# Two unused gaps in SBUF that move where a kernel's split activations begin

## The chip, the cores and the metric

The kernel runs on one core of one Trainium2 chip. The metric is the time of one execution on the device in microseconds (us), the median of several runs. Durations of single instructions are in nanoseconds (ns).

## What is computed

Two small transformer-like models in a row, two layers each, in float32, batch 1. The first has 256 tokens and 16 learned tokens ahead of them (272 in all), the second the 256 alone; the width is 1024. A layer is a mixer (gated linear attention, a sparse attention, a gated recurrence, a banded attention) and a feed-forward block. The change touches the operands of three products:

```python
def swiglu(h, w_in, w_out):                  # both layers of the first model, D_FF = 2816
    gate, up = jnp.split(h @ w_in, 2, axis=-1)
    return (jax.nn.silu(gate) * up) @ w_out

# the end of gla_mixer, layer 0 of the first model
    o = rmsnorm(o, g_out.reshape(GLA_HEADS, GLA_DV)).astype(h.dtype).reshape(B, T, D_MODEL)
    return (o * jax.nn.silu(r)) @ w_out
```

## The kernel before

Activations lie transposed in SBUF: the 128 partitions hold features, the free dimension holds tokens, and a tensor of 1024 features is eight rows one behind the other in each partition. Weights come as a stream of units of 128x1024 numbers (512 KB) through a ring of four slots, in the order in which they are used (`PHASES`).

**Split products.** To keep float32 accuracy, each operand of a large product is split into a high part of type float32r and a low part, the rest. ScalarE makes `w_hi` from `w_raw` (L511), VectorE makes `w_lo` (L1679), and the activations are split likewise. Each 128x128 tile of a unit then takes three matmuls with the weights as the stationary and the activations as the moving operand:

```python
wh = w_hi[:, slot, n * P:(n + 1) * P]
wl = w_lo[:, slot, n * P:(n + 1) * P]
nc.tensor.matmul(out, wh, xh[:, k, tok], start=first and n == 0, stop=False)   # L1004
nc.tensor.matmul(out, wh, xl[:, k, tok], start=False, stop=False)              # L1005
ins = nc.tensor.matmul(out, wl, xh[:, k, tok], start=False, ...)               # L1006
```

One unit is 24 such matmuls. `xh` and `xl` are `x_hi` and `x_lo` for most products, and tensors of their own for others:

- `ga_hi`, `ga_lo`: the gated output of the linear attention, 8 rows (k) of 272 tokens, made at L617 and L1860, read by the product `gla_out`: 8 rows x 3 matmuls x 8 output tiles = 192 matmuls of 272 columns.
- `mid_hi`, `mid_lo`: the middle of the gated feed-forward block, 22 rows, made tile by tile at L653 and L1905 while the first product of the block still runs, read by `ffn0_out` (272 columns) and `ffn1_out` (256 columns): 22 x 3 x 8 = 528 matmuls in each of the two layers.
- `m_hi`, `m_lo` (the second model's feed-forward blocks), `at_*`, `xq_*`, `c_*`, `lr_*` alike.

**Where things lie.** SBUF tensors are laid out one behind the other in each partition, each size rounded up to 32 bytes. What is used in one stage only lies in a region that every stage reuses from the same address (`region()`): one for the linear attention, one for the gated feed-forward block, one for the sparse attention, and so on. So a tensor's place follows from the sizes ahead of it in its own region. Tensors named `..._pad` are never read or written. The rows of `x`, `ga` and `mid` are 320 numbers (1280 bytes, five times 256) apart, of which 272 or 256 are used, so that every row starts at the same place past a multiple of 256 bytes; those of `m`, `at`, `xq` and `lr` are 1024 bytes apart. Two exceptions: row 7, the last of `x_hi` and `x_lo`, lies 64 bytes further, and the rows of `c_hi` and `c_lo` are 1088 bytes apart. `xs_hi` is the same tile as `x_hi` with the 256 tokens' first at the row's start; where `x_hi` itself is read for the 256 tokens alone, reading begins 64 bytes further, past the 16 learned tokens. In the program as built this gives, for the moving operands, in bytes past a multiple of 256:

| operand | columns | start |
|---|---|---|
| `mid`, `ga` | 272 or 256, 272 | 64 |
| `m`, `at`, `xq` | 256 | 64 |
| `x` in the first model's full products (rows 0 to 6; row 7) | 272 | 64; 128 |
| `xs` (rows 0 to 6; row 7) | 256 | 64; 128 |
| `x` in `dsa_qidx` and `dsa_q` (rows 0 to 6; row 7) | 256 | 128; 192 |
| `c_hi`, rows 0 and 1 (L1274, L1276) | 272 | 64, 128 |
| `c_lo`, rows 0 and 1 (L1275) | 272 | 192, 0 |
| `k2rs_hi`, `k2rs_lo` (L1500, L1501) | 256 | 96 |

The stationary operands `w_hi` and `w_lo` start 128 bytes past a multiple of 256, tile by tile 512 bytes apart.

**Order.** Every engine's order is written out by hand, with semaphores between the engines. TensorE waits for `lo_ready` (weights split) and for the activations' split at a stage's start, ScalarE and VectorE wait for `units_used` and `acc_free`, by which TensorE gives back a ring slot and an output bank is handed on, and SP reloads a slot when VectorE has split it.

Of the kernel before, what the change touches and what calls it, by code (L numbers as in the profile page):

```python
# [21 lines left out]
P = 128  # L22
# [131 lines left out]
def build(nc, hT, weights, cols, w_a2, bias1_rows, bias2_rows, constants, outT):  # L154
    ctx = ExitStack()
    with ctx:
# [37 lines left out]
        def region():  # L194
            stack = ExitStack()

            def get(name, shape, dt=F32):
                return stack.enter_context(nc.sbuf_tensor(name, shape, dt))
            return stack, get


        stack, get = region()
        ga_hi = get("ga_hi", [P, KD, ROW], F32R)
        ga_lo = get("ga_lo", [P, KD, ROW], F32R)
        k_T = get("k_T", [P, 4, T])
# [21 lines left out]
        stack, get = region()  # L227
        gate_s = get("gate_s", [P, 2, T])
        up_s = get("up_s", [P, 2, T])
        silu_s = get("silu_s", [P, 2, T])  # L230
        mid_s = get("mid_s", [P, 2, T])
        mid_hi = get("mid_hi", [P, 24, ROW], F32R)
        mid_lo = get("mid_lo", [P, 24, ROW], F32R)
        sqg = get("sqg", [P, KD, T])
# [3 lines left out]
        stack, get = region()  # L238
# [30 lines left out]
        stack, get = region()  # L269
# [15 lines left out]
        stack, get = region()  # L285
# [7 lines left out]
        stack, get = region()  # L293
# [2244 lines left out]
def program(nc, arrays):  # L2538
    args = [nc.dram_tensor(n, a.shape, mybir.dt.from_np(a.dtype), kind="ExternalInput").ap()
            for n, a in arrays.items()]  # L2540
    out = nc.dram_tensor("outT", (P, KD, SEQ), F32, kind="ExternalOutput").ap()
    build(nc, *args, out)
# [12 lines left out]
```

## Time and profile before

| | before |
|---|---|
| median of 3 runs | 1182.88 us |
| runs | 1182.33 to 1183.76 us |
| span of the profiled execution | 1182.2 us |
| PE busy | 1169.6 us, 99% |
| DVE busy | 819.2 us, 69% |
| ACT busy | 691.5 us, 58% |
| DMA | 207.84 MB, mean 176 GB/s |

The profiled execution has no time of its own beside its span; the span lies 0.7 us under the median of the runs. PE is TensorE's matmuls, PEld its weight loads, DVE VectorE, ACT ScalarE, POOL GpSimd. Matmuls are pipelined, so the records of successive ones overlap: a matmul's record is about 163 ns longer than the distance from its start to the next one's start. The distance is what one matmul costs in a stream.

### The profile page before, as it was taken

What the parts mean: (1) busy time and instruction counts of PE and PEld (TensorE: products, weight loads), DVE (VectorE), ACT (ScalarE), POOL (GpSimd) and SP (SyncE); (2) the same over time, 40 slices, a digit from 0 to 9 for tenths busy, and PEclk for the clock granted to TensorE, in tenths of its full rate; (3) what the DMA queues carried; (4) which work ended last, traced back from release to release, by engine and by line L of the source; (5) the groups of instructions that cost most, each with busy time, mean ns of one, the idle gap of its engine ahead of it and who ended that gap; (6) DMA issues with size and microseconds to landing.
All of it is one profiled execution on the core that took longest, in us unless ns stands there. A gap on an engine that the chain in (4) does not pass through costs nothing. (4 is left out here: it accounts for less than half of the span.)

```text
span 1182.2 us, 25988 instructions
## 1 busy us (share of the span) xinstructions
PE 1169.6 (99%) x9738; PEld 1140.9 (97%) x9738; DVE 819.2 (69%) x1296; ACT 691.5 (58%) x1115; POOL 89.5 (8%) x97
## 2 busy tenths in 40 slices
PE   8999999999999999999999999999999999999998
PEld 8999999999998899999999989999999979999998
DVE  7767866665577877666668997675567677776543
ACT  6635765654455567666556976664447576666432
POOL 1000200000110020000120000000013223000000
PEclk9999999999999999999999999999999999999999
DMA  7532655555664336555664556666666424566663
GB/s 270 177 94 89 193 178 177 177 178 192 200 202 144 107 107 190 191 190 193 209 209 155 193 180 192 191 193 191 206 212 205 142 77 153 185 193 193 202 195 106
DMA packets 57577, 207.84 MB, mean 176 GB/s; under 512 B 6352, under 2 KB 7568, under 8 KB 57248
## 3 DMA queue, kind: packets, MB, share of 16 engines
q1 hardware_dynamic: 57136, 203.52, 54.6%
q0 software_dynamic: 288, 3.21, 0.7%
q8 instruction: 54, 0.88, 0.3%
q14 instruction: 19, 0.16, 0.0%
q10 hardware_dynamic: 80, 0.07, 0.0%
HBM read 205.66 MB, written 1.05 MB: 175 GB/s over the span
## 5 line engine op out<-in xcount | busy, mean ns | idle before, releaser
L1679 DVE TENSOR_TENSOR w_lo<-w_raw,w_hi 128x1024 fp32r<-128x1024 f32 x379 | 463.4, 1225 | 68.7 <-ACT w_hi L511 68.1
L511 ACT CAST w_hi<-w_raw 128x1024 fp32r<-128x1024 f32 x379 | 395.1, 1045 | 174.1 <-PE acc L1006 172.2
L1004 PE MATMUL acc<-x_hi,w_hi 128*128 128x256 f32 (+1 forms) x1688 | 479.0, 284 | 2.2 <-DVE w_lo L1679 1.5
L1005 PE MATMUL acc<-x_lo,w_hi 128*128 128x256 f32 (+1 forms) x1688 | 473.3, 280 | 0.0
L1006 PE MATMUL acc<-x_hi,w_lo 128*128 128x256 f32 (+1 forms) x1688 | 473.2, 280 | 0.0
L1004 PEld LDWEIGHTS acc<-x_hi,w_hi 128*128 128x128 f32 x1688 | 317.8, 188 | 6.0 <-DVE x_lo L1699 1.8
L1005 PEld LDWEIGHTS acc<-x_lo,w_hi 128*128 128x128 f32 x1688 | 317.7, 188 | 0.5
L1006 PEld LDWEIGHTS acc<-x_hi,w_lo 128*128 128x128 f32 x1688 | 317.6, 188 | 0.0
L1004 PE MATMUL acc<-m_hi,w_hi 128*128 128x256 f32 x512 | 141.3, 276 | 0.0
L1005 PE MATMUL acc<-m_lo,w_hi 128*128 128x256 f32 x512 | 141.3, 276 | 0.0
L1006 PE MATMUL acc<-m_hi,w_lo 128*128 128x256 f32 x512 | 141.3, 276 | 0.0
L1004 PE MATMUL acc<-mid_hi,w_hi 128*128 128x272 f32 (+1 forms) x352 | 99.0, 281 | 0.0
L1006 PE MATMUL acc<-mid_hi,w_lo 128*128 128x272 f32 (+1 forms) x352 | 99.0, 281 | 0.0
L1005 PE MATMUL acc<-mid_lo,w_hi 128*128 128x272 f32 (+1 forms) x352 | 99.0, 281 | 0.0
L1006 PEld LDWEIGHTS acc<-m_hi,w_lo 128*128 128x128 f32 x512 | 96.1, 188 | 0.0
L1004 PEld LDWEIGHTS acc<-m_hi,w_hi 128*128 128x128 f32 x512 | 96.1, 188 | 0.0
L1005 PEld LDWEIGHTS acc<-m_lo,w_hi 128*128 128x128 f32 x512 | 96.1, 188 | 0.0
L1006 PEld LDWEIGHTS acc<-mid_hi,w_lo 128*128 128x128 f32 x352 | 66.2, 188 | 0.0
L1004 PEld LDWEIGHTS acc<-mid_hi,w_hi 128*128 128x128 f32 x352 | 66.2, 188 | 0.0
L1005 PEld LDWEIGHTS acc<-mid_lo,w_hi 128*128 128x128 f32 x352 | 66.2, 188 | 0.0
L887 ACT ACTIVATE y_s<-y_s 128x256 f32<-128x256 f32 x64 | 26.8, 419 | 63.3 <-DVE y_s L2304 62.9
L526 ACT ACTIVATE sq<-h 128x256 f32<-128x256 f32 (+1 forms) x64 | 26.3, 420 | 57.9 <-DVE h L1714 47.8
(370 smaller groups left out, 1671.3 us busy)
## 6 DMA issues: line engine op xcount, KB each, us to landing
w_raw<-weights SPq DMA_DIRECT2D x381, 512.0 KB, 4.0
bias<-bias_rows POOLq DMA_DIRECT2D x1, 2048.0 KB, 8.7
h<-hT SPq DMA_DIRECT2D x4, 272.0 KB, 4.5
bias<-bias_rows POOLq DMA_DIRECT2D x1, 1088.0 KB, 8.9
outT<-h SPq DMA_DIRECT2D x4, 256.0 KB, 4.6
con<-constants SPq DMA_DIRECT2D x1, 913.0 KB, 9.3
w_raw<-weights SPq DMA_DIRECT2D x2, 256.0 KB, 3.1
par<-cols SPq DMA_DIRECT2D x1, 84.0 KB, 2.0
```

Of the source, the lines that this page charges most:

```text
L511: nc.scalar.copy(w_hi[:, slot, :], w_raw[:, slot, :]).then_inc(hi_ready, 1)
L526: nc.scalar.activation(sq[:, nn, tok], h[:, nn, tok], ACT.Square).then_inc(sq_ready, 1)
L887: nc.scalar.activation(y2_s[:, j % 2, :], y_s[:, j % 2, :], ACT.Square).then_inc(s_("y2_ready"), 1)
L1004: nc.tensor.matmul(out, wh, xh[:, k, tok], start=first and n == 0, stop=False)
L1005: nc.tensor.matmul(out, wh, xl[:, k, tok], start=False, stop=False)
L1006: ins = nc.tensor.matmul(out, wl, xh[:, k, tok], start=False, stop=last and n == ntiles - 1)
L1679: V.tensor_tensor(w_lo[:, slot, :], w_raw[:, slot, :], w_hi[:, slot, :].bitcast(F32), ALU.subtract)\
```

## The change

Two tensors that nothing uses are put into two of the regions. `ga_pad` takes 32 bytes in each partition at the start of the linear attention's region, `mid_pad` 128 bytes in the feed-forward region, between `mid_s` and `mid_hi`.

```diff
         stack, get = region()
+        ga_pad = get("ga_pad", [P, 8])
         ga_hi = get("ga_hi", [P, KD, ROW], F32R)
         ga_lo = get("ga_lo", [P, KD, ROW], F32R)
         k_T = get("k_T", [P, 4, T])
...
         mid_s = get("mid_s", [P, 2, T])
+        mid_pad = get("mid_pad", [P, 32])
         mid_hi = get("mid_hi", [P, 24, ROW], F32R)
         mid_lo = get("mid_lo", [P, 24, ROW], F32R)
         sqg = get("sqg", [P, KD, T])
```

No instruction is added, removed or moved on any engine; only addresses differ. In the built program `mid_hi` and `mid_lo` start at 192 past a multiple of 256 instead of 64, and `sqg` behind them moves by the same 128 bytes. `ga_hi` and `ga_lo` start at 96 instead of 64, and all that lies behind them in the linear attention's region (`k_T`, `v_T`, `q_T`, `r_T`, `a1_T`, `z` and its fellows, `k_tok`, `v_tok`, `S`, `o_T` and so on) moves by 32 bytes. The other regions, the weights' ring and `x` stay where they were.

## Rows read from the trace of the kernel before

**Rows 1.** The page's part 1: busy us, share of the span, instructions.
```profile
PE 1169.6 (99%) x9738; PEld 1140.9 (97%) x9738; DVE 819.2 (69%) x1296; ACT 691.5 (58%) x1115; POOL 89.5 (8%) x97
```

**Rows 2.** Windows, PE alone: stretch, length, busy (instructions in it), clock, DMA.
```profile
core 0: us, PE busy (x), PEclk, DMA share, GB/s
270.00:330.00 60.00, 60.00 (x488) 1.00 0.62 197
567.00:622.00 55.00, 55.00 (x488) 1.00 0.66 211
119.00:134.00 15.00, 15.00 (x124) 1.00 0.68 221
150.00:260.00 110.00, 110.00 (x890) 1.00 0.57 177
450.00:560.00 110.00, 110.00 (x966) 1.00 0.59 188
800.00:870.00 70.00, 70.00 (x620) 1.00 0.63 193
```

**Rows 3.** Groups of matmuls by line and shape: count | busy us, mean ns | idle before.
```profile
L1004 PE MATMUL acc<-mid_hi,w_hi 128*128 128x272 f32 x176 | 50.4, 287 | 0.0
...
L1004 PE MATMUL acc<-mid_hi,w_hi 128*128 128x256 f32 x176 | 48.6, 276 | 0.0
...
L1004 PE MATMUL acc<-ga_hi,w_hi 128*128 128x272 f32 x48 | 13.8, 286 | 0.0
```

**Rows 4.** Groups of all engines in the stretch of `ffn1_out`, 564.3 to 623.9.
```profile
L1679 DVE TENSOR_TENSOR w_lo<-w_raw,w_hi 128x1024 fp32r<-128x1024 f32 x24 | 30.2, 1281 | 2.5 <-ACT w_hi L511 2.5
L511 ACT CAST w_hi<-w_raw 128x1024 fp32r<-128x1024 f32 x24 | 25.0, 1047 | 14.0 <-PE acc L1006 14.0
...
L1714 DVE TENSOR_TENSOR h<-h,acc 128x256 f32<-128x256 f32 x7 | 3.0, 422 | 15.3 <-PE acc L1006 15.3
```

**Rows 5.** Timeline of PE in `dsa_qidx`: start us, length, engine, line, names.
```profile
343.63 0.28 PE L1004 MATMUL acc<-x_hi,w_hi 128*128 128x256 f32 x1
...
345.07 0.28 PE L1004 MATMUL acc<-x_hi,w_hi 128*128 128x256 f32 x1
...
345.43 0.29 PE L1004 MATMUL acc<-x_hi,w_hi 128*128 128x256 f32 x1
...
347.95 0.28 PE L1004 MATMUL acc<-x_hi,w_hi 128*128 128x256 f32 x1
```

**Rows 6.** Timeline of PE in `ffn0_in`, from row 7 of one unit on.
```profile
201.07 0.28 PE L1004 MATMUL acc<-x_hi,w_hi 128*128 128x272 f32 x1
...
201.45 0.29 PE L1004 MATMUL acc<-x_hi,w_hi 128*128 128x272 f32 x1
...
204.04 0.28 PE L1004 MATMUL acc<-x_hi,w_hi 128*128 128x272 f32 x1
```

**Rows 7.** Timeline of PE in the products of `c`; six matmuls from the first row to the last.
```profile
373.34 0.29 PE L1275 MATMUL acc<-c_lo,w_hi 128*128 128x272 f32 x1
...
374.08 0.29 PE L1275 MATMUL acc<-c_lo,w_hi 128*128 128x272 f32 x1
```

**Rows 8.** Timeline of PE where `k2rs` is spread; four matmuls to the last row.
```profile
920.19 0.29 PE L1500 MATMUL pa<-k2rs_hi,hbrd 128*128 128x256 f32 x1
...
920.67 0.28 PE L1004 MATMUL acc<-xq_hi,w_hi 128*128 128x256 f32 x1
```

**Rows 9.** Groups of matmuls in one unit of `q2`, 917.3 to 919.8.
```profile
L1004 PE MATMUL acc<-xq_hi,w_hi 128*128 128x256 f32 x8 | 2.2, 281 | 0.0
```

**Rows 10.** Groups of matmuls of the linear attention by line and shape, whole span.
```profile
L1135 PE MATMUL acc<-q_T,S 128*128 128x64 f32 x64 | 7.6, 271 | 0.0
...
L1122 PE MATMUL pa<-v_tok,k_tok 64*128 64x256 f32 x16 | 5.2, 477 | 0.2 <-DVE v_tok L1799 0.2
```

## The prediction

> **What bounds the kernel now.** The page's busy shares come first: TensorE is busy 99% of the span, VectorE 69%, ScalarE 58% [rows 1]. The kernel is a stream of matmuls, and its time is their number times the distance between two starts. The change adds no instruction, so I ask two things: is the distance set by TensorE itself in the three stages that read the moved operands, and does it depend on where the moving operand begins?
>
> For the first, windows over the two feed-forward output products and the linear attention's show PE busy for their whole length, at a granted clock of 1.00 (the level of 2.4 GHz) [rows 2]. The groups of `ffn1_out` show who waits: VectorE stood idle 15.3 us and ScalarE 14.0 us for TensorE's matmuls, and the matmuls have no idle time [rows 3, 4]. DMAs were busy 62 to 68% [rows 2]. So whatever a matmul gains or loses there goes into the span one to one, 528 times in each layer and up to 192 times in `gla_out`. Longer matmuls only make the two other engines wait longer; nothing behind them becomes late.
>
> The distances at the present start of 64 bytes follow from the windows, where about two of the counted instructions straddle an end: 60 us over 486 is 123.4 ns for `mid` with 272 columns, 55 over 486 is 113.2 ns for `mid` with 256, 15 over 122 is 123 ns for `ga`, and 70 over 618 is 113.3 ns for `m` [rows 2]. The bare columns at 2.4 GHz are 113.3 and 106.7 ns, so 10 and 6.6 ns come on top at this start.
>
> **The second question, from the rows that happen to start elsewhere.**
>
> 256 columns at 128 bytes: in `dsa_qidx` rows 0 to 6 of `x` start at 128. From 343.63 to 345.07 there are 12 matmuls: 120 ns each. Same line, same weights' place, same column count as the 113.2 ns at 64.
>
> 256 columns at 192 bytes, the new place of `mid`: row 7 of the same products. Its three matmuls take from 345.07 to 345.43, again 120 ns each, and the 24 of the next whole unit, from 345.07 to 347.95, are 2.88 us, 120 ns each with row 7 in them [rows 5]. If row 7 took 113 ns, 20 ns would be missing there. So 192 costs what 128 does: 6.7 ns more than 64.
>
> A second look at 128: the long stream of `xs` (450 to 560) has only row 7 at 128. 110 us over 964 is 114.1 ns on the mean, 0.9 more than 113.2; over 24 matmuls that is 21 ns, 7 for each of the three of row 7 [rows 2]. It agrees.
>
> 272 columns at 128 bytes: row 7 in `ffn0_in`. Its three matmuls take 0.38 us (127 ns each) [rows 6], and the window's mean of 110 over 888, 123.9 ns, against 123.4 gives 24 x 0.5 / 3 = 4 ns more for each [rows 2]. I take 127.
>
> 272 columns at 192: only `c_lo`'s first row. A run of six (two at 64, two at 128, one each at 192 and 0) takes 0.74 us [rows 7]. Less 2 x 123.4 and 2 x 127, there are 240 ns for the two at 192 and 0 together. If the one at 0 costs its bare columns, 113.3, the one at 192 costs 127; if both cost the same, 120. So the bounds are 120 and 127, or with the largest row for this shape, rounding in, 128. I take 126, near the upper end, because with 256 columns 192 costs as much as 128.
>
> 272 columns at 96: no row. It lies between 64 (123.4) and 128 (127). The nearest row is `k2rs` with 256 columns at 96: four matmuls in 0.48 us, 120 ns [rows 8], but in a stretch where operands at 64 run slow too (below). I take 2 ns more, bounds 0 and 4.
>
> **The sum.**
> - `ffn1_out`: 528 x 6.7 ns = 3.5 us. If the stream settles at the 118 ns of rows 9, 2.5.
> - `ffn0_out`: 528 x (126 - 123.4) = 1.4 us; bounds 528 x (-3.4) = -1.8 and 528 x 4.6 = 2.4.
> - `gla_out`: 192 x 2 ns = 0.4 us; bounds 0 and 0.8. Its first 48 matmuls wait for `ga_ready` anyway.
> - the linear attention's other operands, moved by 32 bytes: their main matmuls are 7.6 and 5.2 us [rows 10]; 6% of that, the largest effect of a start seen above, is 0.8 us either way. They lie among waits between engines. I take 0.
> - ScalarE's and VectorE's writes of `mid` and `ga` and GpSimd's reads of `sqg` start elsewhere too. I take 0: in the stages that use them TensorE is waited for, 14 to 15 us of it [rows 4], which is the cover; a tenth more on each would not use it up.
>
> Sum +5.3 us. The profiled span would go from 1182.2 to 1187.5, and since the runs' median stands 0.7 us above the span, the median from 1182.88 to 1188.2. The ends of the terms give 2.5 - 1.8 - 0.8 = -0.1 and 3.5 + 2.4 + 0.8 + 0.8 = 7.5: 1182.8 to 1190.4.
>
> **A rule that speaks against it.** The rows say that two streams of 256 columns in the same line differ by 6.7 ns with the start alone. The Trainium skill, page "TensorE: Matmul & The Clock Gate", section "Back-to-back issue gap", gives the distance as columns over 2.4 plus 2.5 ns, with no term for where the operand begins; by it nothing would change. Its page "SBUF — State Buffer", section "Door 1: The DMA port swizzle", has lines of 16 bytes, and 64, 96, 128 and 192 are all multiples of 16; by that too nothing would change. That is the second rival below, whose price is zero.
>
> **The rivals.**
> 1. *Another start is better for 272 columns (faster).* The run of `c` allows it: if a start at 0 costs 123.4 like one at 64, the one at 192 costs 117, and `ffn0_out` gains 528 x 6.4 = 3.4 us. Against the 3.5 us lost in `ffn1_out` that alone comes out even. It ends faster only if 192 with 256 columns costs less than 64 + 1.9 ns or so, that is, if row 7's 120 ns in rows 5 is only the neighbours' pace carried over, since three matmuls between two groups at 120 may not show their own cost. With 113.2 there the time is 1182.9 - 3.4 = 1179.5 us. For it: row 7 is never seen in a stream of its own. Against it: rows 5 has it to the nanosecond at 120, and in the stream of `xs` three odd matmuls do leave their trace. 8%.
> 2. *The start does nothing by itself (same).* The 120 ns of rows 5 would be due to something else in that stage, or three even effects cancel: the cheaper 120 ns in `ffn0_out` (-1.8) and the stream of rows 9 in `ffn1_out` (+2.5). For it: one unit of `q2` reads `xq` at 64 and shows records of 281 ns, 118 between starts, against 276 and 113 elsewhere [rows 3, 9], so the same operands can run at two paces, and the start is not the whole story. Against it: the stream in rows 5 is even, and row 7 of `xs` shows the step in every unit. Time 1182.9 to 1184. 14%.
> 3. *The pace falls further.* If 192 with 272 columns clashes with the weights' load, as 134 ns rather than 126, `ffn0_out` loses 5.6 us and the sum is 9.5: 1192.4 us. Nothing but single distances speaks for it. 5%.
>
> My forecast, 1184.5 to 1190.5 us, has the remaining 73%.
>
> **How the numbers follow.** A change of 0.2%, 2.4 us, is about what a measurement of this kernel can tell from none; it lies at 1185.2 and 1180.5. The predicted time is the likeliest case, 1188.2. The forecast and the third rival count as slower (78%), the second rival as the same (14%), the first as faster (8%). The range from 1182.8 to 1191.0 takes in the bounds of the terms and most of the second rival.
>
> **What the changed profile would show.** The group of L1004 with `mid` at 256 columns at 283 ns instead of 276, and 55 us from inside `ffn1_out` holding some 460 matmuls instead of 488. `mid` at 272 at about 289 or 290 instead of 287. `ga` at 288 instead of 286. Every stretch with `x`, `m`, `at` or `xq` the same as before, shifted. VectorE's and ScalarE's waits for TensorE in `ffn1_out` each longer by a few us. The prediction is wrong if `mid` at 256 columns stays at 276 (row 7's 120 was then the neighbours'), if the group at 272 columns falls below 287, or if the linear attention between 62 and 111 us changes its length by over 1 us.

## The result, and the profile after

The changed kernel takes 1188.68 us in the median of four runs (1187.33 to 1188.83), against 1182.73 us for the kernel before: a ratio of 1.0046, with a 95% interval from 1.0034 to 1.0059, or 4.0 to 7.0 us more. The profiled execution of the changed kernel has a span of 1185.3 us; its own time was 1187.33 us.

Windows over PE in the changed kernel, in the order of [rows 2] (stretch, length, busy with the count of instructions in it, granted clock, DMA). The fourth to sixth are streams that the change doesn't touch:

```profile
core 0: us, PE busy (x), PEclk, DMA share, GB/s
270.00:330.00 60.00, 60.00 (x476) 1.00 0.61 189
567.00:622.00 55.00, 55.00 (x469) 1.00 0.63 202
119.00:131.00 12.00, 12.00 (x98) 1.00 0.66 215
150.00:260.00 110.00, 110.00 (x890) 1.00 0.56 176
450.00:560.00 110.00, 110.00 (x966) 1.00 0.61 188
800.00:870.00 70.00, 70.00 (x620) 1.00 0.64 197
```

PE is busy for the whole of each stretch, as before, but fewer matmuls fit into the first three. Two of each count straddle an end again, so the distances are 60 / 474 = 126.6 ns for `mid` with 272 columns (123.4 before), 55 / 467 = 117.8 ns with 256 (113.2 before) and 12 / 96 = 125 ns for `ga` (123 before). The other three counts are those of [rows 2] to the unit. The groups of matmuls by line and shape say the same: 289, 279 and 288 ns where [rows 3] have 287, 276 and 286:

```profile
L1006 PE MATMUL acc<-mid_hi,w_hi 128*128 128x272 f32 x176 | 50.9, 289 | 0.0
...
L1006 PE MATMUL acc<-mid_hi,w_hi 128*128 128x256 f32 x176 | 49.1, 279 | 0.0
...
L1006 PE MATMUL acc<-ga_hi,w_hi 128*128 128x272 f32 x48 | 13.8, 288 | 0.0
```

The groups of the other engines in `ffn1_out` (564.6 to 626.7 us) show that what a matmul gained in length went into waits for it, against [rows 4]:

```profile
L513 ACT CAST w_hi<-w_raw 128x1024 fp32r<-128x1024 f32 x24 | 25.0, 1046 | 15.8 <-PE acc L1008 15.8
L1716 DVE TENSOR_TENSOR h<-h,acc 128x256 f32<-128x256 f32 x7 | 3.0, 422 | 17.2 <-PE acc L1008 17.2
```

Their work is as long as before, 1046 and 422 ns each, and both wait about 2 us more. So the account of the matmuls is 528 x 3.2 = 1.7 us, 528 x 4.6 = 2.4 us and 192 x 2 = 0.4 us: 4.5 us. (Taken over whole streams the distances are 126.66 against 123.34, 117.78 against 113.35 and 125.3 against 123.4 ns, with the same sum.)

The two profiled spans differ by 3.1 us only. Most of the difference to 4.5 is in the linear attention, where the granted clock fell in the execution of the kernel before that was profiled. The window from 68 to 72 us, first of before, then of the changed kernel (busy time of PE, PEld, DVE, ACT, POOL, then clock and DMA):

```profile
68.00:72.00 4.00, 4.00 (x21) 2.97 (x20) 2.78 (x8) 0.00 (x0) 0.00 (x0) 0.57 0.19 76
```
```profile
68.00:72.00 4.00, 4.00 (x36) 3.56 (x33) 2.49 (x7) 0.00 (x0) 0.00 (x0) 1.00 0.15 61
```

At a clock of 0.57 on the mean, so mostly at the level of 1.2 GHz, TensorE got 21 matmuls into the stretch instead of 36; the group of L1122 in [rows 10], 477 ns on the mean, is 389 ns in the changed kernel:

```profile
L1124 PE MATMUL pa<-v_tok,k_tok 64*128 64x256 f32 x16 | 4.0, 389 | 0.2 <-DVE v_tok L1801 0.2
```

From the last matmul of `x` ahead of the linear attention (59.73 and 59.52 us) to the first of `ga` (111.18 and 109.35) the first profile needs 51.45 us, the second 49.83. The kernel before, profiled again in experiment 1, needs 49.83 too, with the clock up. So the drop comes and goes from execution to execution of one kernel, and is no part of the change. Why it came isn't shown.

### The profile page after: what moved, and what is told of

Its sections match the earlier page's. It is cut to its first block and busy times, and to the rows that moved or that the text cites. A ratio compares the mean times of both kernels' runs of the same rounds, so it can differ in the third digit from the quotient of the medians.

```text
span 1185.3 us, 25988 instructions
## 1 busy us (share of the span) xinstructions
PE 1171.6 (99%) x9738; PEld 1143.1 (96%) x9738; DVE 819.3 (69%) x1296; ACT 691.3 (58%) x1115; POOL 89.3 (8%) x97
## 5 line engine op out<-in xcount | busy, mean ns | idle before, releaser
L1716 DVE TENSOR_TENSOR h<-h,acc 128x272 f32<-128x272 f32 (+1 forms) x32 | 13.7, 429 | 70.2 <-PE acc L1008 69.2
```

Of the source, the lines that this page charges most:

```text
L1716: V.tensor_tensor(h[:, n, tok], h[:, n, tok], acc[n % 4][:, 0:n_tok], ALU.add).then_inc(acc_free, 1)
```

## The experiments

Twelve kernels were run, each compared with the kernel before on the same chip. Distances below are worked out from windows like those above, or from the same trace's starts over the whole stream. "Difference" is the moving operand's start less the stationary operand's, in bytes, modulo 256; in the kernel before it is 64 - 128, so 192, for nearly all streams. That 256 is a fitting measure shows in [rows 2] and the whole streams: the rows of `m` are 1024 bytes apart, those of `mid` 1280, and both have 113.35 ns.

**1. The kernel before once more (`again`).** No edit.

> The kernel before, run as if it were a change, for a measure of what no change looks like. Every theory: ratio 1.000 within 0.001. It also tells whether the time outside the profiled span (0.5 us for the kernel before, 2.0 us for the changed one) and the drop of the granted clock at 68 to 72 us belong to one kernel or come and go from run to run: if they come and go, spans here vary by about 1.4 us and the rest outside the span is not always 0.5 us.

Measured: 1183.73 us in the median of 12 runs against 1183.35 of 25; ratio 1.0001 (0.9992 to 1.0009). Single spans went from 1180.7 to 1183.1 us. The time outside the span was 1.8 to 3.0 us in these runs and 1.9 to 3.5 in those of the kernel before beside them, mostly 2.0, so it belongs to no kernel. The clock did not fall at 68 us in this profile, whose span was 1181.0 us. A stream that nothing changed ran slower here than in the first profile: the one of `xq` at 988 us, with 14 / 119 = 118 ns instead of 113.3:

```profile
988.00:1002.00 14.00, 14.00 (x121) 1.00 0.70 225
```

The first two profiles differ in this way as well, where the change moved nothing: over 48 matmuls of `xq` at 907 us before and 910 us after, the mean distance is 115.3 and 119.4 ns.

**2. Each gap alone (`mid192_only`, `ga96_only`).**

```diff
+        mid_pad = get("mid_pad", [P, 32])      # the first kernel: this line alone
+        ga_pad = get("ga_pad", [P, 8])         # the second kernel: this line alone
```

> Only the split middle's gap of 128 bytes. Theory A (a matmul's distance to the next depends on where its moving operand begins): 126.7 ns in the first layer and 117.8 ns in the second as in the changed kernel, so 1.7 + 2.4 = 4.1 us more than before, and the linear attention as before. Rival (other shifted operands of the linear attention carry much of it): under 3 us.

> Only the gap of 32 bytes ahead of the gated output. Theory A: 144 matmuls of the stream at 125.3 instead of 123.3 ns and 48 gated ones alike, 0.3 to 0.4 us in all, so a ratio of 1.0003, not told from 1. Rival (the time outside the span, or the linear attention's other operands, cost 1.5 us with this gap): 1.0012 or more, with the product itself at the same 125.3 ns.

Measured: the middle's gap alone 1187.46 us against 1183.35, ratio 1.0029 (1.0018 to 1.0039), and in the profile the changed kernel's two distances to the hundredth (126.66 and 117.77 ns). The gated output's gap alone 1184.46 us, ratio 1.0004 (0.9996 to 1.0013), not told from no change; from the last matmul of `x` to the first of `ga` it has the 49.83 us of the kernel before, so the linear attention's other operands cost nothing. But in its own stream it ran slower than in the changed kernel, with the same addresses: 16 / 127 = 126 ns where that had 125; and `at`, which doesn't move, took 16 / 136 = 118 ns where before it took 113. Windows of `ga96_only` over the two:

```profile
117.00:133.00 16.00, 16.00 (x129) 1.00 0.66 210
427.00:443.00 16.00, 16.00 (x138) 1.00 0.67 210
```

So the middle carries 4.1 of the 4.5 us, and a stream can have two paces at one pair of addresses.

**3. The middle at a multiple of 256 (`mid0`).**

```diff
+        mid_pad = get("mid_pad", [P, 48])
         mid_hi = get("mid_hi", [P, 24, ROW], F32R)
```

> A gap of 192 bytes ahead of the split middle, which then starts at a multiple of 256. Theory A with the sum over the run of c (240 ns for a start at 192 and one at 0 together, of which 192 took 126.7): 113.3 ns for 272 columns and at most 113.3 for 256, so 5.3 us less than before in the first layer and 0 to 3.5 us less in the second. Rival (start 64 is the best one, any other costs more): at least as long as before, 123.4 and 113.3 ns or more.

Measured: 1189.21 us against 1183.35, ratio 1.0041 (1.0026 to 1.0056), and 60 / 474 = 126.6 ns with 272 columns, 55 / 464 = 118.5 with 256:

```profile
270.00:330.00 60.00, 60.00 (x476) 1.00 0.60 189
570.00:625.00 55.00, 55.00 (x466) 1.00 0.63 204
```

Theory A's sum over the run of `c` falls: a start at 0 isn't cheap.

**4. The middle at 128, and its two parts apart (`mid128`, `hi192_lo64`).**

```diff
+        mid_pad = get("mid_pad", [P, 16])      # mid128: high and low part at 128
```
```diff
+        mid_pad = get("mid_pad", [P, 32])      # hi192_lo64
         mid_hi = get("mid_hi", [P, 24, ROW], F32R)
+        mid_pad2 = get("mid_pad2", [P, 32])
         mid_lo = get("mid_lo", [P, 24, ROW], F32R)
```

> The split middle starts at 128 past a multiple of 256. Theory A (the moving operand's start alone sets the distance, and row 7 and the sparse attention's products of the kernel before are good samples of a start at 128): 120.0 ns with 256 columns, 127 to 128 ns with 272, so 528 x 6.7 + 528 x 4.2 = 5.8 us more than before. Rival C (a stream has a few paces and keeps the one it falls into, whatever the start): 118 and 125 to 127, 4 us or less.

> The high part starts at 192, the low part stays at 64. Two of three matmuls read the high part. If each matmul pays for its own start: two thirds of the changed kernel's 3.3 and 4.4 ns, so mean distances of 125.5 and 116.3 ns, 2.7 us more than before. If the stream's pace is set as a whole by its worst operand: 126.7 and 117.8 ns, 4.1 us.

Measured: `mid128` 1.0037 (1.0024 to 1.0049), with 60 / 479 = 125.3 ns and 55 / 459 = 119.8:

```profile
270.00:330.00 60.00, 60.00 (x481) 1.00 0.62 193
570.00:625.00 55.00, 55.00 (x461) 1.00 0.62 200
```

The 120 ns of the sparse attention's stream are met with 256 columns, but 272 columns stay below the 127 ns that a lone row 7 showed in `ffn0_in`, so theory A is wrong there, and rival C is wrong with 256 columns. `hi192_lo64` 1.0028 (1.0013 to 1.0044), with 124.5 ns for 272 columns, below the two thirds that were expected, and 117.8 ns for 256, the whole of the changed kernel's. Neither expectation fits both: a stream of mixed starts needn't run at the mean of its parts' distances. (With 256 columns the low part may have had the 117.8 ns that its unmoved start can have too, as in experiment 1; with 272 columns no such reading is left.)

**5. The weights' ring moved, the activations left (`ring192`, `ring64`).** The region's tensors and `x` keep their places; `w_raw`, `w_hi`, `w_lo` and `h` shift together. Of these TensorE's split products read only `w_hi` and `w_lo`; no run moves them alone.

```diff
+        w_pad = sb("w_pad", [P, 16])           # ring64: [P, 48]
         w_raw = sb("w_raw", [P, RING, TILES * P])
...
-        x_pad = sb("x_pad", [P, 48])
+        x_pad = sb("x_pad", [P, 32])           # ring64: no x_pad
```

> The weights' ring (w_raw, w_hi, w_lo, and h behind it) moves by 64 bytes to 192 past a multiple of 256; every activation operand stays at its start. Theory A: all distances as before, time as before within 0.1%. Theory B (what counts is the moving operand's start less the stationary's, which here becomes 128 for all streams, as it was for the middle at 0): 126.7 ns with 272 columns and 118.7 with 256 in all streams, about 8,400 matmuls by 4 ns, 35 us more. Anything between says that both starts count on their own.

> The weights' ring starts at 64 past a multiple of 256, like most activations. Theory A: as before within 0.1%. Theory B (the difference becomes 0, as it is for the sparse attention's x at 128 against weights at 128): 120 ns with 256 columns and 127 with 272 in all streams, 50 us more; the sparse attention's products then have a difference of 64, as the changed kernel's middle, and fall from 120 to 118.

Measured: 1215.20 us against 1183.76 (1.0265; 1.0248 to 1.0282), and 1219.86 us (1.0301; 1.0284 to 1.0318). No split activation has moved, and the distance of all the streams has. Windows of `ring192` over `x` with 272 columns, `x` with 256, `mid` and `m`, and of `ring64` over the same:

```profile
150.00:260.00 110.00, 110.00 (x870) 1.00 0.55 174
455.00:565.00 110.00, 110.00 (x928) 1.00 0.58 182
578.00:630.00 52.00, 52.00 (x441) 1.00 0.65 206
815.00:885.00 70.00, 70.00 (x592) 1.00 0.60 186
```
```profile
150.00:260.00 110.00, 110.00 (x881) 1.00 0.55 174
455.00:565.00 110.00, 110.00 (x919) 1.00 0.58 181
578.00:630.00 52.00, 52.00 (x436) 1.00 0.64 203
815.00:885.00 70.00, 70.00 (x586) 1.00 0.61 184
```

`m` takes 70 / 590 = 118.6 ns with the ring at 192, a difference of 128, which is the distance of `mid0`, whose difference is also 128; and 70 / 584 = 119.9 ns with the ring at 64, a difference of 0, which is the distance of `mid128`. With 272 columns `ring192` has 110 / 868 = 126.7 (as `mid0`) and `ring64` 110 / 879 = 125.1 (as `mid128`). The sparse attention's products, whose `x` starts at 128, become faster where the others become slower: in the trace of `ring192`, at a difference of 192, 114.3 ns instead of 120, in that of `ring64`, at 64, 117.8 and, in a shorter second stream, 115.7. Theory A is out. Theory B fits all the long streams of these two kernels but one: `ga`, 272 columns at a difference of 0, took 16 / 126 = 127 ns in `ring64` (126.6 over the whole stream) where `x` and `mid` took 125.2 and 125.3:

```profile
118.00:134.00 16.00, 16.00 (x128) 1.00 0.68 214
```

It is the same slower value that `ga` showed in `ga96_only`. The times rose by 31 and 36 us, less than the 35 and 50 expected: B's price for a difference of 0 had been taken too high (127 ns instead of 125.3 with 272 columns), about 7,800 matmuls are in these streams and not 8,400, and `x` with 256 columns started from 114.2 ns, not 113.3.

**6. Row 7 of `x` in line with the others (`row7_in_line`).**

```diff
-LAST_ROW_SHIFT = 16
+LAST_ROW_SHIFT = 0
```

> Row 7 of x_hi and x_lo no longer lies 64 bytes further, so all rows start at 64 and differ from the weights' start by 192 like the others. Theory B (the difference of the two starts sets the distance): x streams at 123.3 ns instead of 123.9 (72 units of 24) and 113.3 instead of 114.2 (132 units), 1.0 + 2.8 = 3.7 us less than before, ratio 0.9968. Rival (the cost belongs to the last row for another reason, such as the end of a unit): no change.

Measured: 1194.15 us against 1184.02, ratio 1.0096 (1.0074 to 1.0118), and single runs from 1189.01 to 1201.27 us, more spread than any other kernel here. Theory B's price for row 7 is met in some streams: `x` with 272 columns ran at 110 / 892 = 123.3 ns instead of 123.9. But the total went the other way, and the rival's "no change" falls too. The first window is over that stream, the next four over streams with 256 columns, all at a difference of 192: `x` in `ffn1_in`, `mid`, `x` in the second model, and `x` in its second layer:

```profile
150.00:260.00 110.00, 110.00 (x894) 1.00 0.57 177
450.00:560.00 110.00, 110.00 (x936) 1.00 0.59 183
570.00:625.00 55.00, 55.00 (x469) 1.00 0.62 202
720.00:790.00 70.00, 70.00 (x619) 1.00 0.63 196
1015.00:1085.00 70.00, 70.00 (x620) 1.00 0.61 189
```

Of the four, the first two run at 110 / 934 = 117.8 and 55 / 467 = 117.8 ns from end to end, the other two at 113.4 and 113.3. The difference of the starts, the column count and the granted clock are alike. So this difference has two paces, 113.3 and 117.8 ns, and a stream keeps the one it falls into; here `at`, `x` and `mid`, one behind the other, all had the slow one. With row 7 in its odd place, every profile of a kernel with the ring at 128 has those long `x` streams at the fast pace, also `ga96_only` and `mid0`, where `at` ahead of them was slow as here. The window of `ga96_only` over `x`:

```profile
450.00:560.00 110.00, 110.00 (x966) 1.00 0.62 191
```

So the odd row costs about 20 ns per unit, and with it a slow pace didn't last into `x`. That it is the row that ends it rests on one profile without it; how it would do that isn't shown. The profiled execution is also the fastest of the five, at 1189.01 us: what made the others 5 to 12 us longer was not seen.

**7. The middle at 32 and at 96 (`mid32`, `mid96`).** As in 3, with gaps of `[P, 56]` and `[P, 8]`.

> The split middle starts at 32 past a multiple of 256, a difference of 160 from the weights. So far a difference of 192 gives 113.3 and 123.3 ns, 128 gives 118.7 and 126.7. If 192 is the best of all: about 116 and 125 ns between them, 2.3 us more than before. If the distance has its least value between them: under 113.3 or 123.3 ns.

> The split middle starts at 96 as the gated output did in the changed kernel: difference 224. With 272 columns 125.3 or 126.7 ns, the two paces seen for the gated output; with 256 columns between those of 192 (113.3) and of 0 (120.0), about 117: 1.0 to 1.8 us and about 2 us more than before.

Measured: `mid32` 1.0013 (1.0004 to 1.0023), 123.3 ns and 55 / 469 = 117.3; `mid96` 1.0037 (1.0025 to 1.0048), 125.3 ns and 118.3. Neither beats a difference of 192 with either column count.

**8. The changed kernel with the ring moved after the middle (`ring0_mid192`).**

```diff
+        w_pad = sb("w_pad", [P, 32])
         w_raw = sb("w_raw", [P, RING, TILES * P])
...
-        x_pad = sb("x_pad", [P, 48])
+        x_pad = sb("x_pad", [P, 16])
```

> The changed kernel with the weights' ring moved too, from 128 to a multiple of 256, so that the split middle at 192 has its old difference of 192 back, while the streams that stay at 64 get a difference of 64. Theory B: the middle returns to 123.3 ns in the first layer and to 113.3 (or 117.8, the second pace of this difference) in the second, though it lies where it made the changed kernel slow; the x and m streams take the changed middle's 126.7 and 117.8 ns, about 30 us more than before in all. Theory A: the middle stays at 126.7 and 117.8 and the others at 123.9 and 114.2.

Measured: 1205.49 us against 1184.63 (1.0176; 1.0159 to 1.0193). Windows over `x` with 272 columns, `mid` with 272, `x` with 256, `mid` with 256, and `m`:

```profile
150.00:260.00 110.00, 110.00 (x872) 1.00 0.55 174
275.00:335.00 60.00, 60.00 (x489) 1.00 0.62 195
455.00:565.00 110.00, 110.00 (x937) 1.00 0.60 185
573.00:628.00 55.00, 55.00 (x488) 1.00 0.64 209
810.00:880.00 70.00, 70.00 (x597) 1.00 0.60 187
```

The middle lies exactly where the change had put it and is back at 60 / 487 = 123.2 and 55 / 486 = 113.2 ns, while `x` and `m`, which lie where they always did, take the changed middle's 117.8 and about 126.4 ns. The slowdown has been handed over whole. The rise of 21 us is what the distances add up to: 2928 x 3.6 ns for `x` with 256 columns, 1536 x 4.4 for `m`, 1464 x 2.5 for `x` with 272 and 192 x 3.2 for `ga`, 21.6 us in all; the 30 expected were added up too high. At this difference too a stream can have the fast pace: `at` took 113.5 ns. And no sum of a price for the activations' start and one for the weights' gives these distances: with the ring at 128 the move of `mid` from 64 to 192 costs 4.4 ns with 256 columns, and with the ring at 0 the operand at 192 is 4.4 ns cheaper than the one at 64.

The distances in ns by difference, from the streams above:

| difference | seen in | 272 columns | 256 columns |
|---|---|---|---|
| 192 | before; ring0_mid192's middle | 123.3 | 113.3 or 117.8 |
| 224 | mid96, ga96_only, after | 125.3, or 126.6 (`ga` in ga96_only) | 118.3 |
| 0 | mid128, ring64 | 125.3, or 126.6 (`ga` in ring64) | 120.0 |
| 64 | after, mid192_only; ring0_mid192's x | 126.7 or 126.4 | 117.8, or 113.5 (`at` in ring0_mid192) |
| 128 | mid0, ring192 | 126.7 | 118.7 |
| 160 | mid32 | 123.3 | 117.3 |

## Why the prediction was right, and where not

**Direction and bound: right.** It had TensorE as what sets the time in the three stages, the cost as a longer distance between matmuls, and no cover for it; all three are in the windows and waits above.

**The total is partly luck.** 5.3 us were forecast; the median rose by 5.95, and the matmuls of the profile account for 4.5, inside the ratio's interval. So the sum was 0.8 us too high and the median of four runs 1.4 us above the matmuls' account, and that the forecast median (1188.2) came within 0.5 us of the measured one is these two together. Where the 1.4 us lie isn't shown; twelve executions of one kernel in `again` spread over 2.7 us.

**The term of `ffn1_out` was mis-sized**: 3.5 us forecast, 2.4 measured (2.5 was its lower bound). The step that failed is "192 costs what 128 does", taken from row 7 in [rows 5]. Three matmuls at another start between two groups at 120 ns kept the neighbours' pace on the mean; in a stream of its own the same pair of starts ran at 117.8 (after) against 120.0 (`mid128`). The objection stood in the first rival, which took the true distance to be 113.2 ns then; it lies between the two.

**The term of `ffn0_out` was right by luck**: 1.4 us forecast, 1.7 measured, 126 ns against 126.7. It rested on dividing up the run of `c`, with a start at 0 as the cheap one. `mid0` shows 126.7 ns at 0, and six matmuls at the stream values would take 2 x 123.3 + 2 x 125.3 + 126.7 + 126.7 = 751 ns, where [rows 7] have 740. Mixed runs don't add up.

**The term of `gla_out` was right**: 0.4 us, 125.4 ns forecast and 125.3 found, though `ga96_only` shows that 126.6 was as possible, and the forecast was a guess between two starts. The linear attention's other operands, taken at 0, cost nothing: 49.83 us in `again`, in the changed kernel and with each gap alone.

**The signs.** `mid` at 256 columns showed 279 ns and 469 matmuls, not 283 and some 460; `mid` at 272 and `ga` the 289 and 288 ns that were named. One sign of being wrong did come up: the linear attention changed its length by more than 1 us (51.45 to 49.83). That is the clock in the first profile and not the change, as `again` shows. And not every stretch of unmoved operands was as before (`xq`, under experiment 1).

**The question was put too narrowly.** "Does it depend on where the moving operand begins?" has the answer yes only because the weights' start was the same in the rows that carried the sum. `ring192`, `ring64` and `ring0_mid192` show that what counts is the moving operand's start less the stationary's. The prediction named the weights' place as a thing held equal, and didn't ask what it does.

**The reading of the time beside the span was wrong**, without harm to the forecast: the 0.7 us compared a profiled execution in which the clock had fallen with the median of others. The time outside the span is about 2 us in the runs that have both.

**The rivals.** The second (two paces at one pair of addresses) described something real: in `again`, `ga96_only` and `row7_in_line` streams at unchanged addresses run at 117.8 instead of 113.3 ns. Since 117.8 is also what the changed `mid` shows with 256 columns, that term alone could be such a switch of pace; but `mid` at 192 has 117.8 in all three profiles of it against a ring at 128 (`after`, `mid192_only`, and with the low part at 64 `hi192_lo64`) and 113.4 in `ring0_mid192`. The unmoved `mid` has 113.4 in the first profile, `again` and `ga96_only`, and 117.8 only in `row7_in_line`, behind a slow `x`. With 272 columns no `mid`, `x` or `ga` at a difference of 192 ran at anything but 123.3 to 123.9 ns. So the rival was wrong in concluding that the start does nothing. The first needed a cheap 192 with both shapes and the third 134 ns; neither occurred.

**The rules by which nothing would change.** The Trainium skill, page "TensorE: Matmul & The Clock Gate", section "Back-to-back issue gap", has no term for addresses; the runs have 113.3 to 120.0 ns for one shape. The formula that the prediction took from it (columns over 2.4 plus 2.5 ns, by which an estimate for 256 columns is 109.2 ns) is given there for an isolated matmul; for a stream with weight loads the section says that both operations set the spacing, again without addresses. The prediction's second rule, by lines of 16 bytes, doesn't tell the starts apart either: all those tried are multiples of 32. The same page of the Trainium skill on TensorE, section "Step-by-step: what each phase is for", says that weight loads and the moving operand come through two independent read ports, so that loading doesn't take bandwidth from the running matmul. Here moving the ring, with every split activation left in place, cost 31 to 36 us, and where `mid` is cheap depends on where the ring lies. So in these streams of split float32 tiles, each matmul with a weight load of its own (9738 of both in [rows 1]), the places of the two operands act together. That the two reads get in each other's way is the likely reading, but what they meet in isn't shown by any run.

## What to carry to other kernels

Where TensorE is busy throughout and every matmul has its own weight load, the places of the two operands can be worth some per cent of a stream (up to 6% here, 113.3 against 120.0 ns): count matmuls in a window of fixed length, and try the difference of the two starts, not each start alone. A lone sample inside another stream doesn't give the size of such an effect; here row 7 gave the sign alone, and the run of `c` gave even the sign of a start at 0 wrong. And streams with a second pace make runs differ: take the distance from each profile before a microsecond is put down to an edit.

## What was not expected of the hardware

A difference of 192 bytes has two stable paces with 256 columns, 113.3 and 117.8 ns, at a granted clock of 1.00, and a stream of hundreds of matmuls keeps one of them (934 in a row in `row7_in_line`, whose `x` has no odd row). With one row in eight at another start, dearer by itself, the kernel is 10 us faster in the median (1184.02 against 1194.15 us) than with all rows at the best start.
